# Latent attention: output panels of two heads, heads 0 and 1 projected in their own group

## What is computed

```python
def mla_mixer(h, ...):
    proj = h @ w_in                       # (L, 256 + 2048)
    c_q = rmsnorm_2(proj[..., :256], q_latent_norm)
    z = proj[..., 256:]                   # one gate for each of 16 x 128 features
    q = (c_q @ w_q_up).reshape(B, L, 16, 192)
    ...
    o = causal_block_attention(q_nope, q_rope, k_nope, k_rope, v).reshape(B, L, 2048)
    return (o * silu(z)) @ w_out          # (2048, 1024)

h = h + rmsnorm_2(y, post_norm[layer])    # the last thing computed
```

## Time and profile before

| what | us |
|---|---|
| median of 3 runs | 1943.84 (1940.74 to 1944.12) |
| the profiled execution's own time | 1942.34 |
| its span, first to last instruction | 1939.6 |
| PE busy in the span | 1833.5 (95%) |
| DVE / ACT / POOL busy | 994.7 / 822.8 / 676.4 |
| PE's share of the chain that ended last | 44% |

### The profile page before, as it was taken

How to read it: one execution, slowest core, us unless ns; L and a number is a source line. 1 busy time by engine, 2 the same in 40 slices (tenths; PEclk the granted TensorE clock), 3 DMA queues, 4 the chain that set the end, 5 groups by cost and what they waited for, 6 DMA issues and landing times.

```text
span 1939.6 us, 30688 instructions
## 1 busy us (share of the span) xinstructions
PE 1833.5 (95%) x11693; PEld 1538.4 (79%) x11829; DVE 994.7 (51%) x1753; ACT 822.8 (42%) x1503; POOL 676.4 (35%) x429
## 2 busy tenths in 40 slices
PE   6999999999999998998999999999978999999996
PEld 4777788888787876887989998998976667777776
DVE  6522233731111225665765774775766556566666
ACT  4566643352323233633633642562445443333433
POOL 3222244453534342270280263255224212222312
PEclk9999999999999998999999999999999999999998
DMA  5112133232323230420230131122132101221201
GB/s 186 55 55 66 55 98 109 66 98 68 118 80 105 86 99 21 137 79 1 80 89 23 55 91 48 52 80 78 34 111 76 55 33 55 65 55 53 76 32 44
DMA packets 73668, 138.90 MB, mean 72 GB/s; under 512 B 30640, under 2 KB 42416, under 8 KB 73296
## 3 DMA queue, kind: packets, MB, share of 16 engines
q1 hardware_dynamic: 72976, 132.41, 22.7%
q10 hardware_dynamic: 576, 4.87, 0.6%
HBM read 127.62 MB, written 9.63 MB: 71 GB/s over the span
## 4 chain that ended last, share of the span: by engine, by line
PE 44%; DVE 6%; POOL 5%; issue 3%; ACT 3%; DMA 0%; SPq 0%; ACTq 0%; POOLq 0%; DVEq 0%
PE ps L348 9%; PE ps L350 8%; PE ps L349 8%; PE ps L3092 4%; PE ps L3048 2%; POOL wsp L343 2%; PE ps L3055 2%; PE ps L3082 1%; POOL ov L836 1%; PE ps L2770 1%; POOL work L832 1%; PE ps L2874 1%; PE ps L2907 1%; PE ps L2912 1%; DVE aux_f L1789 1%
## 5 line engine op out<-in xcount | busy, mean ns | idle before, releaser
L343 POOL TENSOR_TENSOR wsp<-raw,wsp 128x1024 fp32r<-128x1024 f32 x228 | 549.8, 2418 | 1154.7 <-ACT wsp L338 1154.5
L348 PE MATMUL ps<-h_split,wsp 128*128 128x264 f32 (+2 forms) x1552 | 535.0, 345 | 16.8 <-DVE h_split L497 5.0
L349 PE MATMUL ps<-h_split,wsp 128*128 128x264 f32 (+2 forms) x1552 | 516.0, 332 | 0.0
L350 PE MATMUL ps<-h_split,wsp 128*128 128x264 f32 (+2 forms) x1552 | 515.6, 332 | 0.0
L348 PEld LDWEIGHTS ps<-h_split,wsp 128*128 128x128 f32 x1552 | 294.3, 190 | 58.2 <-issue 17.2
L349 PEld LDWEIGHTS ps<-h_split,wsp 128*128 128x128 f32 x1552 | 295.3, 190 | 28.8 <-issue 0.2
L350 PEld LDWEIGHTS ps<-h_split,wsp 128*128 128x128 f32 x1552 | 294.2, 190 | 29.2
L338 ACT ACTIVATE wsp<-raw 128x1024 fp32r<-128x1024 f32 x228 | 237.6, 1050 | 95.2 <-PE ps L350 94.5
L348 PE MATMUL ps<-y_split,wsp 128*128 128x512 f32 (+2 forms) x512 | 196.4, 384 | 11.5 <-DVE y_split L531 5.3
L349 PE MATMUL ps<-y_split,wsp 128*128 128x512 f32 (+2 forms) x512 | 192.5, 376 | 0.0
L350 PE MATMUL ps<-y_split,wsp 128*128 128x512 f32 (+2 forms) x512 | 192.0, 375 | 0.0
(11 more groups left out here) (391 smaller groups left out, 2929.6 us busy)
## 6 DMA issues: line engine op xcount, KB each, us to landing
raw<-in_w SPq DMA_DIRECT2D x228, 512.0 KB, 3.5
m_home<-ov SPq DMA_DIRECT2D x16, 256.0 KB, 3.5
x_home<-x_res ACTq DMA_DIRECT2D x1, 2112.0 KB, 6.9
x_res<-in_x SPq DMA_DIRECT2D x4, 512.0 KB, 5.3
out<-x_res SPq DMA_DIRECT2D x16, 128.0 KB, 1.7
x_res<-x_home ACTq DMA_DIRECT2D x1, 1584.0 KB, 7.4
mats<-in_mats SPq DMA_DIRECT2D x1, 640.0 KB, 7.4
x_res<-x_home ACTq DMA_DIRECT2D x1, 528.0 KB, 3.9
```

The source lines that it names most:

```text
L343: pool.tensor_tensor(wsp[:, s, 1, :], raw[:, s, :], wsp[:, s, 0, :].bitcast(F32), ALU.subtract).then_inc(lo_ready, 1)
L348: pe.matmul(o, wh, xh, start=start, stop=False)
L349: pe.matmul(o, wh, xl, start=False, stop=False)
L350: return pe.matmul(o, wl, xh, start=False, stop=stop)
```

## The change

The output weights now come in panels of two heads instead of four. A tile of the output projection is two `mm3` blocks (6 matmuls) instead of four, and there are twice as many: a group's heads 0 and 1 ("out") are projected in slots 12 to 15 of their own group, two tiles in each slot, and its heads 2 and 3 ("late") in slots 4 to 7 of the next group, or in the tail after the last. The gate tiles 2 and 3 move to slots 8 to 11; in the first group, which has no late part, they are in slots 4, 5, 7 and 8. The gate's exp, clamp, Ln, Exp and product move with them, `gate_y` of heads 0 and 1 comes a slot earlier, and the split of these two heads moves from the next group's begin into slot 11. Each group now has 16 additions (the first 8) where it had 8 (the first none), and they stand at the end of VectorE's slot. The stream has 47 panels instead of 48.

```diff
-MLA_FIRST = 8
-PANELS = P_MLA + 48
+MLA_FIRST = 9
+PANELS = P_MLA + MLA_FIRST + 12 * 3 + 2
...
+        FILLS = {u: ("gate", u // 2, u % 2) for u in range(4)}
+        FILLS.update({u: ("gate", u // 2 - 2, u % 2) for u in range(8, 12)})
+        FILLS.update({u: ("late", 2 * u - 8) for u in range(4, 8)})
+        FILLS.update({u: ("out", 2 * u - 24) for u in range(12, 16)})
+        FILLS_FIRST = {u: f for u, f in FILLS.items() if u < 4 or u >= 12}
+        FILLS_FIRST.update({4: ("gate", 2, 0), 5: ("gate", 2, 1), 7: ("gate", 3, 0), 8: ("gate", 3, 1)})
...
+        def out_adds(g, late, n):
+
+            return gst(g, 16, (0 if late else 8) + n)
...
 # ScalarE
                 if not first:
-                    for t in range(4):
+                    for t in (2, 3):
                         act.activation(YM[:, 0, t, :], mz[t], ACT.Copy).then_inc(sem("z_hi"), 1)
...
-                    if u in (2, 4, 6, 8):
-                        exp_z(u // 2 - 1)
-                    if u in (3, 5, 7, 9):
-                        sigmoid(act, nth_mz(g, (u - 3) // 2), mzsig, mzsig)
+                    if u in (2, 4, 10, 12):
+                        exp_z((2, 4, 10, 12).index(u))
+                    if u in (3, 5, 11, 13):
+                        sigmoid(act, nth_mz(g, (3, 5, 11, 13).index(u)), mzsig, mzsig)
+                    if u == 11:
+                        act.wait_ge(sem("z_y"), gst(g, 4, 18))
+                        for t in (0, 1):
+                            act.activation(YM[:, 0, t, :], mz[t], ACT.Copy).then_inc(sem("z_hi"), 1)
...
-            for p in range(PANELS - 4 + AHEAD, PANELS):
-                split_high(act, p)
...
 # VectorE, slot u, between the maximum and the reciprocal
-                    if u >= 9 and not first:
-                        add_out(u - 9)
...
 # VectorE, at the end of slot u, behind the copy of the transposes
-                    if u in (10, 11):
-                        gate_y(11 - u)
+                    if u in (9, 10):
+                        gate_y(10 - u)
+                    if u == 11:
+                        for t in (0, 1):
+                            low_y(t, gst(g, 4, 17 + t))
+                    kind = fills(first).get(u, ("none",))
+                    if kind[0] in ("late", "out"):
+                        for n in (kind[1], kind[1] + 1):
+                            add_out(kind[0] == "late", n)
...
 # TensorE
+                def fill_out(late, n):
+                    j = out_at(late, n, first)
+                    if n % 4 == 0:
+                        panel_split(j)
+                    if n < 2:
+                        pe.wait_ge(sem("z_copy"), gst(g, 4, 16 + n + (1 if late else 3)))
                     else:
-                        pe.wait_ge(sem("m_add"), gst(g, 8, m - 1))
-                    for kt in range(4):
...
+                        pe.wait_ge(sem("m_add"), out_adds(g, late, n - 1))
+                    for kt in range(2):
+                        t = 2 * late + kt
+                        if n == 0:
+                            pe.wait_ge(sem("z_lo"), gst(g, 4, (15 if late else 17) + kt))
+                        last = mm3(pe, PS[:, FILL[n % 2], :], *part(j, 2 * (n % 4) + kt),
+                                   YM[:, 0, t, :], YM[:, 1, t, :], kt == 0, kt == 1)
+                    last.then_inc(used if n % 4 == 3 else sem("out_half"), 1)
...
 # TensorE, tail_tile
-                for kt in range(4):
+                for kt in range(2):
```

More of the change, by code:

```diff
@@ L2204, in mla_group @@
                            .then_inc(sem("m_nmx"), 1)
[L2205 to L2213, removed]
-                    if u >= 9 and not first:
-                        add_out(u - 9)
+                    if u in (2, 4, 10, 12):
+                        copy_z((2, 4, 10, 12).index(u))
+                    if u in (1, 3) and not first:
+                        low_y(2 + u // 2, gst(g, 4, 15 + u // 2))
+                    if u in (3, 5, 11, 13):
+                        clamp(dve, nth_mz(g, (3, 5, 11, 13).index(u)), mzsig)
+                    if u in (4, 6, 12, 14):
+                        silu_z((4, 6, 12, 14).index(u))
                     if u < 16:
@@ L2238, in _ @@
             mla_loop(dve, mla_group)
-            for t in range(4):
-                low_y(t, 28 + t + 1)
+            for t in (2, 3):
+                low_y(t, 16 * 2 - 3 + t)
             def tail_add(h, m):
@@ L2970, in fill_z @@
                     if half == 0:
-                        panel_split(3 + t)
-                        if t >= 2:
+                        panel_split(z_at(t, first))
+                        if t >= 2 and first:
                             pe.wait_ge(sem("z_copy"), gst(g, 4, 16 + t - 1))
+                        elif t >= 2:
+                            pe.wait_ge(sem("m_add"), out_adds(g, True, 8 + t - 3))
                     for kt in range(4 * half, 4 * half + 4):
-                        last = mm3(pe, PS[:, FILL[t % 2], :], *part(3 + t, kt), HS[:, 0, kt, REAL], HS[:, 1, kt, REAL],
-                                   kt == 0, kt == KT - 1)
+                        last = mm3(pe, PS[:, FILL[t % 2], :], *part(z_at(t, first), kt), HS[:, 0, kt, REAL],
+                                   HS[:, 1, kt, REAL], kt == 0, kt == KT - 1)
@@ L2999, in mla_group, with fill @@
+                def fill(u):
+                    kind = fills(first).get(u, ("none",))
+                    if kind[0] == "gate":
+                        fill_z(*kind[1:])
+                    elif kind[0] != "none":
+                        for n in (kind[1], kind[1] + 1):
+                            fill_out(kind[0] == "late", n)
                 panel_split(0)
@@ L3094, in mla_group @@
                         last.then_inc(sem("m_o"), 1)
[L3095 to L3099, removed]
+                if not first:
+                    panel_split(11)
+                    pe.matmul(PS[:, 7, 0:2], part(11, 0)[0], cq[:, 0, 0, 0:2],
+                              start=True, stop=True).then_inc(used, 1)
             mla_loop(pe, mla_group)
@@ L3181, in host_layout, with mla_out @@
     wo = f["mla_w_out_2"][0]
-    def mla_out(g):
-        return packed(wo[512 * g:512 * (g + 1)])
+    def mla_out(g, late):
+        return packed(wo[512 * g + 256 * late:512 * g + 256 * late + 256])
     for g in range(NG):
```

69 lines of the change are left out of this document (31 added, 38 removed).

## The result

| | before | after |
|---|---|---|
| median | 1943.98 us (1937.88 to 1946.61, 6 runs) | 1956.38 us (1951.81 to 1959.45, 6 runs) |
| the profiled execution's own time | 1942.34 us | 1956.9 us |
| its span | 1939.6 us | 1955.1 us |

The account below looks back on a forecast made before the run. PE was taken to bound the looped groups (104.38 of 106.65 us busy), VectorE the tail's second stage. Tail -8.4, looped groups +12.6, first group +9.75 sum to +13.95 on 1942.34: 1956 us, terms' bounds 1950.5 to 1963, overall range 1946 to 1963.

Parts of the forecast that it names:

- The looped groups: Fills in slots 5, 7, 13, 15 wait for additions, slot 12 for its split: 4.2 us a group, +12.6 for three.
- what queues behind the additions (maximum, exponential): VectorE's later slots: PE does not need this work before the transposes behind the next fill; costed at nothing.
- the hand-over: Looped groups' waits: from VectorE's end of an addition to PE's start of the fill, taken as 0.15 us.
- The tail: After the last group: tiles take 0.72 us instead of 1.44 until VectorE paces; -8.4 us, bounds -9 and -7.5.
- the slow clock at the begin is in it as it is now: Tail's begin: the slow clock stays as before, 0.50 for 3.1 us.
- the two panel splits that go hold nobody: Tail: the two dropped panel splits on GpSimd and ScalarE delay no engine, so no gain was counted.
- The first group: Four fills in slots 12 to 15 +8.15, stalls +2.75, moved gate tile 3 -1.15: +9.75 us.
- The stalls: First group, slots 12, 13 and 15: the same waits as in looped groups, +2.75 us.
- A: Rival, looped groups: the additions hold nobody, since VectorE is half idle; -1.4 us, 1941 us; chance 0.11.
- B: Rival, whole kernel: VectorE binds nowhere, even in the tail; work moves into PE's gaps; -4.5 us, 1937.8 us; chance 0.07.
- C: Rival, first group: the slow clock falls on the fills, costing 2.5 us more, 1959 us; chance 0.08.
- D: Rival, filled slots: waits add up as the late maximum reaches the transposes, 1.2 us at four slots a group; above 1963; chance 0.04.

Follow-up runs that it names:

- experiment 1: The changed kernel with a slot's two additions moved in front of the copy of the transposes: 1947.69 us, ratio 1.0022 to the kernel before.
- experiment 2: The changed kernel with ScalarE's high parts of heads 0 and 1 directly behind slot 11's exponential: 1949.33 us, ratio 1.0033 to the kernel before.
- experiment 3: The changed kernel with both moves, additions before the transposes' copy and high parts behind slot 11's exponential: 1942.88 us, ratio 0.9994 to the kernel before.
- experiment 4: The kernel before with each addition moved to the end of the slot of its own fill: 1944.32 us, ratio 1.0005.
- experiment 5: The kernel before with two of four products per tail output tile, heads 2 and 3 left out, all four panels kept: 1935.14 us, ratio 0.9964.
- Experiment 10: The kernel before with half the tail's products, blocks from the first two panels, the last two panels not split: 1935.21 us, ratio 0.9961.
- experiment 6: The kernel before with 12 unread matmuls of 512 columns in each of the first group's slots 12 to 15: 1954.78 us, ratio 1.0056.
- experiment 9: The kernel before with half the tail's products, blocks from the first two panels, the last two still split: 1936.76 us, ratio 0.9962.
- experiments 7 and 8: Tail edits (head 3 before head 2, second half's sums of squares on GpSimd): on experiment 3's kernel 1940.00 us, on the kernel before 1941.58 us.

## Why the prediction was right, step by step

**The looped groups** (forecast 4.2 us each, measured 3.77). The mechanism is shown: experiment 1 removes the additions' part, experiment 2 the split's, experiment 3 both, and experiment 4 shows that the late place costs nothing while banks alternate slot by slot. By the Trainium skill's rule on rotating banks (Perfetto Trace Analysis, Matmuls) the evacuation of one group should overlap the next one's matmuls. The trace agrees: the banks rotate before and after the change, but a fill whose bank is evacuated too late for that starts 0.54 to 0.66 us later. Each wait was forecast a little long: 0.68 against 0.57 in slot 13, 0.77 against 0.66 in slot 15, the same two against 0.54 and 0.62 in slots 5 and 7, and 1.25 against 1.05 in slot 12; only what follows in slot 12 was forecast short (0.1 against 0.23). For the additions the size that was off is the hand-over: I took the 0.15 us from VectorE's end to PE's start at the tail's begin, and here they are 0.04. In slot 12 I had added full lengths of instructions that follow one another on an engine, where each starts before the one ahead has ended: ScalarE's high parts come 1.36 us behind the output copy, not 1.54. That what queues behind the additions (maximum, exponential) holds up nobody is borne out too: the places named make up 3.67 of the 3.77 us.

**The tail** (forecast -8.4, measured -7.15). Every step up to the first scaling came out within 0.1 us except the begin, which has some 28 matmuls at the slow clock instead of 16 (by the distances between their starts). This length is not set by the change: the kernel before with its additions moved (experiment 4) has 29 slow ones and a tail of 42.49 us, the changed one with its additions moved (experiment 1) 16 and a tail of 33.08. Pairs of like stretches are 42.49 and 34.14 (-8.35), and 41.29 and 33.08 (-8.21). So the size was right and the profiled pair was not alike; from what these runs show, "the slow clock at the begin is in it as it is now" can't be forecast to better than 1.2 us.

One sentence of this step was wrong in its reach: "the two panel splits that go hold nobody". It holds in the tail before and not in a tail of half the work: there they cost 1.7 us (experiments 5, 10). The forecast's -8.4 was not touched, because it had been worked out for a tail without them. For the slow addition of squares the Trainium skill has a rule (SBUF — State Buffer, Who interferes with whom): a VectorE instruction with two inputs in SBUF contends with a GpSimd instruction that reads SBUF. The trace agrees: 2.57 and 2.15 us beside GpSimd's low parts, 0.42 without. The additions of output tiles, with one input in PSUM, stay at 0.42 beside them.

**The first group** (forecast +9.75, measured +9.96). The total was right by luck, from errors that nearly cancel. The fills were sized at 8.15 by comparing a stretch with a slow spell in it (17.50 us) with one without; experiment 6, with the spell on both sides, measured 9.2. On the other side the spell is absent from the changed kernel's first group. That gives back about 0.6 us before slot 12, and 0.4 in it: the scores are 1.0 shorter, but the second half of them now waits 0.57 us for the exponential of an earlier unit (L1475). The stalls are 2.05 us (101.63 against 99.58 in experiment 3), where the forecast had 2.75. From slot 12 on, where experiment 6 gave 9.3, that makes 9.3 - 0.4 + 2.05 = 10.95 of the 11.1 us measured; 10.9 were forecast. Between slots 6 and 12 the group is 23.50 us, before 24.55: -1.05, where -1.15 was forecast, but for a reason that was only half right, since 0.6 of it lies in slots 10 and 11, where the clock had been low, and 0.45 in slots 6 to 9.

**The range.** Added up again, the terms' bounds come out a little wider at the top: 5.7 us a looped group and not 5.6, and 1950.8 to 1963.5 in all, where the prediction has 1950.5 to 1963. The measured time is far from either end.

**The rivals.** A falls by the 14 waits, but is nearly what experiment 3 is: with two groups of lines moved the additions do hold nobody, and the time is 1942.88 against its 1941. B falls in the tail, where PE is busy for 17.39 of 34.14 us and VectorE for 24.02, and the gain is what VectorE's chain allows. The idea behind it, from the Trainium skill (Perfetto Trace Analysis, Optimization Strategy), that interleaving regimes with different bottlenecks may gain, is not borne out for this pair of stretches: the tail gave 8.2 us, and the same columns cost 9.2 in a first group in which PE was already busy for 82.83 of 87.80 us. C went the other way. D did not occur.

What remains open: why the start of the first group moves by up to 5.6 us between profiles of kernels that are alike up to there, what keeps the clock up in the changed first group, and what decides when the clock falls ahead of the tail. No experiment was made on any of them.

## What to carry to other kernels

Count, for a work item that is halved, how many of its buffers the next step wants at once: a late evacuation that was free with one tile a slot costs a wait in every second slot with two, and moving it ahead of an unrelated wait in the same engine's list removes them all. When sizing a wait, take the distance between starts of neighbouring instructions, not the sum of their lengths, and the hand-over from the same pair of instructions where a row has one. When a stretch with a slow clock is compared with one without, take its extra time out first. And what another engine does beside a stage is hidden only as long as the stage keeps its length.

## What the runs showed of the hardware that was not expected

- In all seven profiles of kernels with the old first group (the kernel before and experiments 4, 5, 6, 8, 9, 10) the granted clock is 0.50 for about 3.4 us somewhere between 1553 and 1567 us. In none of the five with the changed first group does it fall there, though slots 9 to 11 are still empty. The change fills slot 8 and leaves slot 6 empty; whether that is the cause was not tested. Experiment 10 had a second spell (0.79 as the mean from 1572 to 1588 us), and a first group of 94.6 us against 91.67.
- Where the tail begins PE is idle for 2.6 us (1.8 in experiments 7 and 8), and the clock falls then or soon after, whatever the kernel. In nine of the twelve profiles it stays at 0.50 for about 3.4 us, in the other three (the changed kernel, experiments 4 and 9) for about 6.8. In these three it fell 1.6 to 2.1 us behind the small matmul, in the nine 2.6 us or more behind it. From 16 to 29 matmuls of 256 columns run slowly, which makes up to some 1.2 us in the time.
- VectorE's sum of two SBUF tiles took 2.57 us instead of 0.42 beside GpSimd's two low parts of 2.37 us each. The second of those ran from 1904.58 (1902.21 + 2.37) to 1906.95 by the row of experiment 5; the sum began 0.08 us behind its start and ended 0.28 behind its end, as if it had waited for all of it. In experiment 9 the sum ended 0.28 us behind the low parts too (1909.28 and 1909.00).
- The scaling of the probabilities (TENSOR_SCALAR, one input, in SBUF) shows the same in the first group and in the looped ones, before and after the change: wherever a low part runs beside it, it ends 0.28 to 0.30 us behind that one. The first row below is of the changed kernel's first group, with no low part at that time; the others are of its first looped group, where the low part ended at 1671.87, 0.29 us ahead of the scaling's end.

```profile
1562.16 0.49 DVE L2245 TENSOR_SCALAR ov<-ov,tiny 128x528 f32<-128x528 f32 x1
...
1669.50 2.37 POOL L343 TENSOR_TENSOR wsp<-raw,wsp 128x1024 fp32r<-128x1024 f32 x1 [9.45 <-ACT wsp L338]
...
1670.34 1.82 DVE L2245 TENSOR_SCALAR ov<-ov,tiny 128x528 f32<-128x528 f32 x1
```
